# Router by pairwise comparison, a token list for two experts first, and expert rows added by the transfer itself

## The reference, cut to what matters

```
g_logits = xt @ w_rg + b_rg                    # 4 groups, the best one is taken
g_w = softmax(g_logits)[g_sel]
e_in = the 4 expert logits of that group       # the best two are taken
top_v, top_i = top_k(e_in, 2)
top_w = softmax(top_v) * g_w
gates[token, expert] = top_w for the two chosen experts, else 0
for e in range(16):
    h = silu(xt @ w_g[e]) * (xt @ w_u[e])      # 1024 -> 512
    out = out + gates[:, e:e+1] * (h @ w_d[e]) # 512 -> 1024
```

## Time and profile before

| | us |
|---|---|
| median of 3 runs | 997.96 |
| lowest and highest run | 993.78, 1000.33 |
| the profiled execution, its own time | 997.03 |
| its span, from first to last instruction | 995.2 |
| PE busy | 895.0 (90%) |
| DVE busy | 657.2 (66%) |
| ACT busy | 490.3 (49%) |

### The profile page before, as it was taken

How to read it: one execution, slowest core, us unless ns; L and a number is a source line. 1 busy time by engine, 2 the same in 40 slices (tenths; PEclk the granted TensorE clock), 3 DMA queues, 4 the chain that set the end, 5 groups by cost and what they waited for, 6 DMA issues and landing times.

```text
span 995.2 us, 14556 instructions
## 1 busy us (share of the span) xinstructions
PE 895.0 (90%) x5884; PEld 511.0 (51%) x5884; DVE 657.2 (66%) x864; ACT 490.3 (49%) x684; POOL 91.7 (9%) x90
## 2 busy tenths in 40 slices
PE   5999999999999998999999989518999999989960
PEld 4434784857656564444444489514545444444420
DVE  3677769533886776443444245454899998988926
ACT  5434373324445444323232325614888878778812
POOL 7000000003000000000000000010121122322100
PEclk9999999999999999999999989758999999999985
DMA  8712414437310115933432260283999999999706
GB/s 206 165 31 63 109 35 114 128 86 149 86 32 17 38 38 193 305 94 96 117 100 83 77 213 2 90 314 131 316 394 388 371 365 376 371 369 366 293 24 251
DMA packets 147247, 174.02 MB, mean 175 GB/s; under 512 B 14391, under 2 KB 99695, under 8 KB 147174
## 3 DMA queue, kind: packets, MB, share of 16 engines
q1 hardware_dynamic: 139760, 158.56, 47.7%
q0 software_dynamic: 7136, 13.89, 5.0%
q10 hardware_dynamic: 278, 0.56, 0.2%
HBM read 168.30 MB, written 13.07 MB: 182 GB/s over the span
## 4 chain that ended last, share of the span: by engine, by line
PE 74%; DMA 11%; DVE 10%; ACT 3%; issue 1%; ACTq 0%; POOLq 0%; DVEq 0%; SPq 0%
PE bank L915 20%; PE bank L916 19%; PE bank L917 19%; DMA arena<-in_moe_wu 6%; DMA arena<-in_moe_wg 4%; PE bank L1127 3%; DVE arena L1645 3%; PE bank L1146 3%; ACT arena L800 1%; PE bank L1021 1%; PE bank L1136 1%; PE bank L1284 1%; DMA arena<-x_rows,token_of 1%; PE bank L1218 1%; PE bank L1006 1%
## 5 line engine op out<-in xcount | busy, mean ns | idle before, releaser
L915 PE MATMUL bank<-arena 128*128 128x512 f16 (+1 forms) x1568 | 465.2, 317 | 13.1 <-DVE arena L1392 4.6
L916 PE MATMUL bank<-arena 128*128 128x512 f16 (+1 forms) x1568 | 464.5, 316 | 0.0
L917 PE MATMUL bank<-arena 128*128 128x512 f16 (+1 forms) x1568 | 464.1, 316 | 0.0
L1645 DVE SCALAR_TENSOR_TENSOR arena<-arena 128x2048 f16<-128x2048 f32 x96 | 216.9, 2288 | 50.2 <-ACT arena L800 50.1
L915 PEld LDWEIGHTS bank<-arena 128*128 128x128 f16 x1568 | 155.1, 99 | 141.5 <-issue 33.8
L917 PEld LDWEIGHTS bank<-arena 128*128 128x128 f16 x1568 | 154.9, 99 | 111.3 <-issue 3.2
L916 PEld LDWEIGHTS bank<-arena 128*128 128x128 f16 x1568 | 154.7, 99 | 99.9 <-issue 3.0
L800 ACT ACTIVATE arena<-arena 128x2048 f16<-128x2048 f32 x96 | 181.5, 1909 | 40.1 <-PE bank L1234 12.5
L567 ACT ACTIVATE arena<-arena 128x1024 f16<-128x1024 f32 (+1 forms) x92 | 92.5, 1007 | 101.3 <-PE bank L917 73.5
L1392 DVE SCALAR_TENSOR_TENSOR arena<-arena 128x1024 f16<-128x1024 f32 (+1 forms) x91 | 103.5, 1163 | 11.4 <-ACT arena L567 9.8
L621 ACT ACTIVATE arena<-bank 128x512 f32<-128x512 f32 x35 | 20.8, 595 | 90.8 <-PE bank L917 90.7
(11 more groups left out here) (257 smaller groups left out, 735.9 us busy)
## 6 DMA issues: line engine op xcount, KB each, us to landing
arena<-in_moe_wg SPq DMA_DIRECT2D x32, 1024.0 KB, 16.4
arena<-in_moe_wu SPq DMA_DIRECT2D x32, 1024.0 KB, 16.3
arena<-in_moe_wd SPq DMA_DIRECT2D x32, 1024.0 KB, 15.3
arena<-in_w_gate SPq DMA_DIRECT2D x32, 512.0 KB, 4.1
arena<-in_w_in SPq DMA_DIRECT2D x31, 512.0 KB, 4.3
arena<-in_w_branch SPq DMA_DIRECT2D x32, 192.0 KB, 3.5
arena<-in_w_out SPq DMA_DIRECT2D x8, 512.0 KB, 5.2
arena<-y_rows SPq DMA_DIRECT2D x4, 1024.0 KB, 8.3
```

The source lines that it names most:

```text
L915: pe.matmul(outb, lhs[0], rhs[0], start=first, stop=False, skip_group_check=True)
L916: pe.matmul(outb, lhs[0], rhs[1], start=False, stop=False, skip_group_check=True)
L917: return pe.matmul(outb, lhs[1], rhs[0], start=False, stop=last_, skip_group_check=True)
L1645: tell("split_done", stt(w_lo[c % NW], stage[c % NS], WSCALE, w_hi[c % NW], ALU.mult, ALU.subtract))
```

## The change

Four things change at once, all in the second half of the kernel.

1. Router. Instead of three calls of `argmax`, every logit of a group is compared with the other three (`is_gt`, and `is_ge` for those that stand lower in the order), the results are summed, and the place of each logit (0, 1, ...) gives group and experts. `sel16` is written before the weights of the two choices are worked out.
2. Token list. The one-hot matrix is first made for experts 0 and 1 alone (NEAR = 2), with 8 small matmuls. The whole one, with its 64 matmuls, moves behind the first two chunks of the expert loop, into the memory where the `xs` rows were.
3. Adding scatter. The residual is stored to HBM (`h_rows`) in eight pieces during the projection, the weight of a choice is put on the result when it leaves PSUM (`slotw`), and POOL's scatter adds into `h_rows`. A scatter waits until the one before it has landed. The end loads `h_rows` back instead of two rows per token.
4. Distances. ACT and DVE split chunk c + 6 at step c (LOOK = 6) instead of c + 5. Stages 8 to 12 are loaded from within the projection loop; before, they stood behind the stores of `x2_rows`. Chunks 5 and 6 are split right after the short token list.

```diff
+LOOK = 6
+NEAR = 2
...
+            for m in range(KD):
+                sp_.wait_ge(S("h_done"), m + 1)
+                sp_.dma_start(h_rows.rearrange("(t p) n -> p t n", p=P)[:, :, m * P:(m + 1) * P], hres[:, :, m * P:(m + 1) * P]
+                              ).then_inc(S("h_stored"), 16)
+                if m - 1 in SPLIT_AT:
+                    c = NS + SPLIT_AT.index(m - 1)
+                    sp_.wait_ge(S("split_done"), c - NS + 1)
+                    stage_load(c)
...
-                sp_.wait_ge(S("split_done"), len(STEPS))
                 for t in range(NT):
-                    sp_.dma_start(yg[t], y_rows.rearrange("(j t p) n -> t p j n", j=2, p=P)[t]
-                                  ).then_inc(S(f"tokens_in{t}"), 16)
+                    sp_.dma_start(hres[:, t, :], h_rows[t * P:(t + 1) * P, :]).then_inc(S(f"tokens_in{t}"), 16)
...
-                        if e >= 2:
-                            pool.wait_ge(S(f"y_stored{e % 2}"), 16 * (e // 2))
-                        pool.indirect_dma_start(out=y_rows, out_offset=bass.IndirectOffsetOnAxis(ap=row_of[:, e:e + 1], axis=0),
-                                                in_=yout[e % 2], in_offset=None, bounds_check=2 * T - 1, oob_is_err=False
-                                                ).then_inc(S(f"y_stored{e % 2}"), 16)
+                        if e >= 1:
+                            pool.wait_ge(S(f"y_stored{(e - 1) % 2}"), 16 * ((e - 1) // 2 + 1))
+                        else:
+                            pool.wait_ge(S("h_stored"), 16 * KD)
+                        pool.indirect_dma_start(out=h_rows, out_offset=bass.IndirectOffsetOnAxis(ap=token_of[:, e:e + 1], axis=0),
+                                                in_=yout[e % 2], in_offset=None, bounds_check=T - 1, oob_is_err=False,
+                                                compute_op=ALU.add).then_inc(S(f"y_stored{e % 2}"), 16)
...
-            act.wait_ge(S("token_full"), 1)
             for c in range(FIRST, NW):
                 split(c)
...
-                    if NW <= c + FIRST < len(STEPS):
-                        split(c + FIRST)
+                    if NW <= c + LOOK < len(STEPS):
+                        split(c + LOOK)
                     if kind == "g" and hf:
                         act.wait_ge(S("chunk_used"), steps_to("g", e))
+                        if e == 0:
+                            act.wait_ge(S("token_full"), 2)
...
+                def all_tokens():
+                    pe.wait_ge(S("onehot_ready"), 1 + NT)
+                    for e in range(NE):
+                        for t in range(NT):
+                            last = pe.matmul(ps[4][:, 4 * e:4 * e + 4], onehot[:, t, :].rearrange("p (c e) -> p e c", e=NE)[:, e, :],
+                                             told[:, t, :, e], start=(t == 0), stop=(t == NT - 1))
+                    last.then_inc(S("token_full"), 1)
...
                     last.then_inc(S("chunk_used"), 1)
+                    if c == 1:
+                        all_tokens()
...
+            link(tt(tied, other, own, ALU.is_ge))
+            link(tt(ahead, other, own, ALU.is_gt))
+            link(tt(tied, tied, lower.rearrange("p (i j) -> p i j", j=EPG).unsqueeze(1).to_broadcast(wide), ALU.mult))
+            link(tt(ahead, ahead, tied, ALU.max))
+            link(dve.tensor_reduce(place[:, 0, :, :, :].rearrange("p t g e -> p (t g) e"), ahead, axis=AX.X, op=ALU.add))
...
+                x_lo(0)
+                dve.wait_ge(S("x2_stored"), 16 * NT)
+                for t in range(NT):
+                    tell("onehot_ready", tt(*onehot_views(t), ALU.is_equal))
                 for c, (kind, e, hf) in enumerate(STEPS):
...
+                    if c == 2:
+                        all_slots()
...
+                def all_slots():
+                    dve.wait_ge(S("token_full"), 2)
...
+                    sig("token_read", tt(slotv[:, 2, :], slotv[:, 2, :], got[:, 3, :], ALU.add))
...
                 def add_rows(t):
                     dve.wait_ge(S(f"tokens_in{t}"), 32)
-                    link(stt(hres[:, t, :], yg[t][:, 0, :], wsel[:, 0, t:t + 1], hres[:, t, :], ALU.mult, ALU.add))
-                    sig("moe_done", stt(hres[:, t, :], yg[t][:, 1, :], wsel[:, 1, t:t + 1], hres[:, t, :], ALU.mult, ALU.add))
+                    sig("moe_done", ts(total[:, 1:2], total[:, 0:1], 1.0, None, ALU.mult))
```

More of the change, by code:

```diff
@@ L158, in constants @@
     sq[:, 2 * P:3 * P] = np.where(r[None, :] > r[:, None], BIG, 0.0)
-    sq[:, 3 * P:3 * P + 4] = np.arange(4, 0, -1)
-    sq[:, 3 * P + 4:3 * P + 8] = r[:, None] + P * np.arange(NT)[None, :]
+    sq[:, 3 * P:3 * P + 4] = r[:, None] + P * np.arange(NT)[None, :]
+    sq[:, 3 * P + 4:3 * P + 20] = np.tril(np.ones((EPG, EPG)), -1).reshape(-1)
     half = np.zeros((P, 2 * P), np.float16)
@@ L283, in build @@
                 .rearrange("p (k c) -> p k c", c=P) for j in range(2)] for i in range(2)]
-        yg = [view(STAGE[t], 2, D) for t in range(NT)]
         nf = arena[:, 8192:8192 + D]
@@ L340, in build @@
         oa_bank = ((ps[6], ps[7]), (ps[4], ps[5]))
-        rt_bank = (ps[6], ps[7], ps[2], ps[3])
-        scratch, x2_rows, y_rows = d["bias_scratch"], d["x2_rows"], d["y_rows"]
+        scratch, x2_rows, h_rows = d["bias_scratch"], d["x2_rows"], d["y_rows"][0:T, :]
         MIXW = 20 + 1 + 1
@@ L433, in _ @@
                 sp_.dma_start(x2_rows[t * P:(t + 1) * P, :], xs[:, t, :]).then_inc(S("x2_stored"), 16)
-            for c in range(NS, NS + FIRST):
-                sp_.wait_ge(S("split_done"), c - NS + 1)
-                stage_load(c)
             sp_.wait_ge(S("dense_known"), 1)
@@ L867, in _ @@
                         act.activation(sgr[e % 2], ps[2 * (e % 2)][:, :], ACT.Tanh, scale=0.5 / WSCALE).then_inc(S("sgr_ready"), 1)
+                        if e == NE - 1:
+                            link(act.activation(stat[:, 2, 0:1], ones[:, 0:1], ACT.Sqrt))
                     if kind == "u" and not hf and e >= 1:
@@ L1217, in _ @@
                     for t in range(NT):
-                        last = pe.matmul(rt_bank[t][:, 0:nr], hgT_f[:, k % 2, t * P:(t + 1) * P], wr[:, k, :],
-                                         start=(k == 0), stop=(k == KD - 1), skip_group_check=True)
+                        last = pe.matmul(ps[6][:, t * nr:(t + 1) * nr], hgT_f[:, k % 2, t * P:(t + 1) * P], wr[:, k, :],
+                                         start=(k == 0 and t == 0), stop=(k == KD - 1), skip_group_check=True)
                     last.then_inc(S("hgT_used"), 1)
@@ L1229, in _ @@
             last.then_inc(S("rank_full"), 1)
-            pe.wait_ge(S("onehot_ready"), NT)
-            for e in range(NE):
+            pe.wait_ge(S("onehot_ready"), 1)
+            for e in range(NEAR):
                 for t in range(NT):
-                    last = pe.matmul(ps[7][:, 3 * e:3 * e + 3], onehot[:, t, :].rearrange("p (c e) -> p e c", e=NE)[:, e, :], told[:, t, :, e],
+                    last = pe.matmul(ps[7][:, 2 * e:2 * e + 2], onehot_near[:, t, :, e], told[:, t, 0:2, e],
                                      start=(t == 0), stop=(t == NT - 1))
@@ L1697, in _ @@
-            link(stt(flat(R(5)), flat(R(6)), BIG, flat(R(4)), ALU.mult, ALU.add))
-            argmax(R(10), R(5), R1(7, 1), R1(0, 1))
-            sig("rt_diff", tt(R1(8), R1(7, 1), R1(7, 0), ALU.subtract))
+            link(dve.tensor_reduce(R1(0), gl, axis=AX.X, op=ALU.max))
+            sig("rt_sub", tt(R(1), gl, R1(0).to_broadcast([P, NT, GROUPS]), ALU.subtract))
+            dve.wait_ge(S("rank_full"), 1)
+            link(dve.tensor_reduce(total[:, 0:1], ps[5][:, NT * NE:(NT + 1) * NE], axis=AX.X, op=ALU.max))
@@ new lines, in _ @@
+            sig("dense_known", ts(dense[:, :], total[0:1, 0:1], float(CAP), None, ALU.is_gt))
+            link(stt(flat(rank[:, :, :]), ps[5][:, 0:NT * NE], 1.0, flat(sel16[:, :, :]), ALU.add, ALU.mult))
+            link(ts(rank[:, :, :], rank[:, :, :], -1.0, None, ALU.add))
+            sig("onehot_ready", tt(onehot_near, slots.rearrange("p (c e) -> p c e", e=NE)[:, :, 0:NEAR].unsqueeze(1)
+                                   .to_broadcast([P, NT, CAP, NEAR]),
+                                   rank[:, :, 0:NEAR].unsqueeze(2).to_broadcast([P, NT, CAP, NEAR]), ALU.is_equal))
@@ new lines, in _ @@
+            link(tt(selj[:, 0, :, :].rearrange("p t (g e) -> p t g e", e=EPG), place[:, 1, :, 1:, :], group, ALU.mult))
+            link(tt(selj[:, 1, :, :], sel16[:, :, :], selj[:, 0, :, :], ALU.subtract))
+            for j in range(2):
+                link(tt(etop[:, j, :, :], elog, selj[:, j, :, :], ALU.mult))
+                link(dve.tensor_reduce(R1(7, j), etop[:, j, :, :], axis=AX.X, op=ALU.add))
+            sig("rt_diff", tt(R1(8), R1(7, 1), R1(7, 0), ALU.subtract))
+            dve.wait_ge(S("token_full"), 1)
@@ L1701, in _ @@
+            near = ps[7][:, 0:2 * NEAR].rearrange("p (e a) -> p a e", a=2)
```

(6 more changed lines are left out.)

112 lines of the change are left out of this document (49 added, 63 removed).

## The result

| | before | after |
|---|---|---|
| median of 11 runs each, us | 997.96 | 1005.22 |
| lowest and highest run | 993.55, 1000.33 | 1002.04, 1005.68 |
| ratio to before, 95% interval | | 1.0081 [1.0063, 1.0099] |
| span of the profiled execution | 995.2 | 1003.4 |

The change made the kernel 0.8% slower, and the time lies outside the range. The profile of after is read in the same order as that of before.

The account below looks back on a forecast made before the run. The prefetched chunks were taken as used up by about 800 us, from where the DMA stream of weights decides. Sum: 997.0 - 12.0 + 2.8 + 9.2 - 10.5 = 986.5, stated as 986 us, range 970 to 1001.

Parts of the forecast that it names:

- start of the stream: Expert loop's start: chunk 16's load goes out at 678.6 instead of 690.56, moving the stream by -12.0 us (-9 to -15).
- distance of 6: Expert loop: while weights are short, step c waits for the split of chunk c + 6, costing +2.8 us (0 to 3.1).
- adding, in the loop: Expert loop: each adding scatter costs a second transfer, 0.7 us each, +9.2 us for 13.
- end: After the last result at 963.96: 20.7 us to the last store instead of 31.2, -10.5 us (-8 to -12).
- DVE's branch: Between token list and first product: DVE's branch taken as 1.6 us, from POOL's 2.1.
- the add is dear: Rival, expert loop: a scatter blocks all engines for about 3.19 us instead of 0.7, giving 1009 (996 to 1015); chance 0.12.
- the point of no gain: Expert loop: from 1.6 us more per scatter, the change would have no gain left.
- The router's part: Logits to first product: list ready at 650.4 instead of 661, first product at 662.6, 12.8 us earlier (10 to 15).
- First product: Start of the expert loop: PE's first expert product at 662.6 us, instead of 675.37.
- PE's idle time: Sign, from 800 us on: some 18 us if the add costs as assumed, about half if it is free.
- the free case: Rival, expert loop: the add's second read overlaps and costs nothing, giving 976 us (971 to 981); chance 0.30.

Follow-up runs that it names:

- look5: The changed kernel with a split distance of 5 instead of 6, nothing else; 1005.87 us.
- no_add_early_look5: The changed kernel with part 3 undone (scatter without adding, old end), DVE reaching its branch early, and a distance of 5 instead of 6; 986.40 us.
- plain: The changed kernel with the scatter overwriting the rows of h_rows instead of adding, every wait kept; 986.66 us.
- twice: The changed kernel with overwriting scatters, each issued twice with the same rows, the second after the first has landed; 1004.77 us.
- quiet: The changed kernel with SP holding back the loads of chunks 13 and 14 until DVE has made the first half of the rows behind its branch; 1002.87 us.
- no_add: The changed kernel with part 3 undone: scatter without adding, choice weights put on at the end, no residual stores; 996.41 us.
- half_adds: The changed kernel with only the scatters of the eight odd experts adding, those of the even ones overwriting; 997.38 us.
- no_branch: The changed kernel without the branch for experts with over 128 tokens, on all five engines; 995.72 us.

## Why the prediction was wrong

The sum said 986.5 and the range ended at 1001. In the profiles, after is 8.2 longer than before:

| term | predicted | came | |
|---|---|---|---|
| start of the stream | -12.0 | -5.4 | 690.56 to 685.12 |
| distance of 6 | +2.8 | 0 to 2.7 | look5, no_add_early_look5 |
| adding, in the loop | +9.2 | +14.2 | stream and rest, after against plain |
| what is left of stream and rest | | +4.0 | plain against before, the distance with it |
| end | -10.5 | -4.5 | 31.2 to 26.7 |

-5.4 + 14.2 + 4.0 - 4.5 = 8.3.

So no single term made the miss. The sum is 18.8 short: 6.6 at the start, of which 5.0 are DVE's branch, 6.0 at the end, 5.0 in the adding, and 1.2 in what else the loop lost. With the adding priced right and nothing else, the sum would still have put the kernel 5.5 us ahead of before, where it is behind.

**The adding scatter: the mechanism was right, the price too low.** A scatter was taken at its share of the software queue, 0.7 us, and the adding as a second one of these. It is a second one, as twice shows, and its own share came close: 0.74 instead of 0.68, and 10.2% where 10.6 was forecast. But a second transfer costs the stream 14.3/13 = 1.1 us, not 0.7. The step that failed here is that bytes are what the engines charge for. A queue's share holds its own packets and not the time that engines stand still around them. The Trainium skill's rule in "Collectives: The Full Stack" (the bandwidth ceiling), half rate for an adding transfer since both reads go through the same ring (given there for the reduce step of a collective), agrees with the measured scatter alone, 6.09 against 3.19. It was a good guide to the transfer, and it doesn't give what the other queue loses.

The rival "the add is dear" had the right side, and its band (996 to 1015) held the time. Its mechanism, 2.5 us per scatter, did not come, and 1.1 is under the 1.6 that it named as the point of no gain. It took the other terms as forecast, and they too came short.

**The router's part held as far as the list**, 8.9 us after the logits as forecast (650.4 - 641.55).

**DVE's branch was mis-sized**: 6.6 instead of 1.6. It was taken a little under POOL's 2.1, and stood on the path. POOL had met its branch with the DMA engines 30% busy; DVE met its own with two loads in flight (62%), which the change itself had moved there and the prediction had not counted. The Trainium skill says in "Runtime: NRT & Kernel Launch" (instruction fetch mechanics) that a taken branch to code outside the window already fetched waits for a DMA fetch of it. That rule bears on this place and was overlooked; it gives no length, and the 3.9 of quiet against 6.6 agree with it. First product forecast 21.0 after the logits, came 25.5; of the 4.5 the branch is 5.0, the rest came 0.5 sooner. From there to chunk 16's load 16.0 were forecast and 15.8 came, with the 64 matmuls at 4.07 instead of 3.1. So the start lost 4.5 to the branch and 2.3 to logits that came late for reasons outside the change. That the branch counts is shown by two times, 8.4 us less without it and 4.3 with it early (by the ratios; the first holds ACT's table loads too). The quiet queue brought chunk 16 forward by 1.4 from the logits, but its time can't be told from after's (0.8 less by the ratios, and the intervals overlap).

**The distance** cost nothing that could be measured in the changed kernel, 2.8 was forecast.

**The end was short by 6.0 us.** 26.7 came instead of 20.7. The scatter is 1.9 of it (6.1 for 4.2). The chain goes through the second of the four loads, which landed 4.9 after the scatter had, where 6.0 were taken for the last. From there to the end it took 13.6 us instead of 8.6: ACT loads its function table for the square root again (991.24, 1.28), and the four rows then go 2.0 apart, one behind the other, where I had counted the last one alone. The 10.4 of additions did go.

**PE's idle time** from 800 us on, 15.4 us, lay between the forecast's 18 and the free case. That reading alone would have called the price right; the loss had begun before 800, at 765 in the chain.

## What to carry to other kernels

Where the DMA engines are full, an adding scatter is two scatters, whatever engine work it saves: here it saved 4.5 us at the end and took 14 in the loop, so it belongs only where the stream has room. Price a transfer by what the stream beside it loses (its own length from first to last load, with one more transfer and without), not by its queue's share alone. And see where each engine meets a branch: work moved ahead of it, and transfers in flight at that time, put its standstill on the path.

## What the runs showed of the hardware

- An adding scatter of an expert's rows lands 5.9 to 6.1 us after issue with nothing beside it, a plain one in 3.2. POOL itself is busy for 2.13 us for one and 1.50 for the other (medians of 16). Packets and bytes in the queue's row are the same.
- DVE stood still for 6.4 to 6.9 us at a branch over the code that isn't taken in six kernels (after, plain, look5, no_add, half_adds, twice), POOL for 2.1. Where DVE came to it 8 us sooner it was at most 4.0, and 3.9 where two loads of weights were held back until it was over.
- ACT loaded a function table, 1.28 us each time, at 978.02 and 991.24 in after, and in no_branch at neither place, with the same functions in the same order there.
- The granted clock of PE fell again after the 64 small matmuls: products of 0.22 before, 0.45 behind them (granted clock 1.00 from 672.7 to 676.1, 0.91 over the 64, 0.55 from 680.2 to 683.2), and once more from 689.8 on (0.50 to 692). Ahead of that stood eight small float32 matmuls (686.63, 1.04 us) and 2.13 us in which PE was idle. The chain of after:

```profile
676.08 0.22 PE bank L932
676.30 3.90 PE bank L1295 x64
680.20 0.45 PE bank L930
...
683.34 0.22 PE bank L932
...
689.79 0.61 PE bank L930
```

It had done products at 2.4 GHz for 3.4 us before, and then matmuls of 4 columns alone.
